# Eight experts in slots of 96 tokens: up weights in rows of 896 columns, gate and up in bank pairs, and POOL's share moved

## The reference

```python
logits = (t @ w_router).astype(jnp.float32) + b_router     # t: 256 tokens x 1024
top_v, top_e = lax.top_k(logits, 2)
gate = jax.nn.softmax(top_v, axis=-1)
...                                 # tokens sorted by expert, in blocks of up to 128
def one(args):                      # per expert: w_gate, w_up 1024 x 3584, w_down 3584 x 1024
    xb, e = args
    return (jax.nn.silu(xb @ w_gate[e]) * (xb @ w_up[e])) @ w_down[e]
...
y = zeros.at[row_tok].add(out * row_g)      # y[token] += gate * expert(token)
```

## Time and profile before

| | |
|---|---|
| median of 3 runs | 2813.24 us (2811.03 to 2813.75) |
| span of the profiled execution, first to last instruction | 2809.8 us |
| median less span | 3.4 us |
| PE, busy in the span | 2745.6 us, 98% |
| DVE | 1982.1 us, 71% |
| ACT | 1608.7 us, 57% |
| POOL | 700.7 us, 25% |
| first expert's first unit on TensorE | about 1876 us |
| last down matmul of the last expert | 2791.32 us |

### The profile page before, as it was taken

One profiled execution on the slowest core, in us unless ns is written; L12 is line 12 of the kernel. 1 busy time (PEld: TensorE's weight loads), 2 busy tenths in 40 slices (PEclk: granted clock), 3 DMA queues, 4 the chain that ended last, 5 costly groups with the idle time before them and its releaser, 6 DMA issues.

```text
span 2809.8 us, 68032 instructions
## 1 busy us (share of the span) xinstructions
PE 2745.6 (98%) x28028; PEld 2292.6 (82%) x28028; DVE 1982.1 (71%) x1914; ACT 1608.7 (57%) x1723; POOL 700.7 (25%) x562
## 2 busy tenths in 40 slices
PE   9999999999999999999999999999999999999997
PEld 7887788888877888887888887888879788797794
DVE  5457575564576755666855566778899898998986
ACT  5445663354356554455643445657677776777765
POOL 4314022122122221120122011144234243242331
PEclk9999999999999999999999999999999999999999
DMA  9764367576643676553576663469999999999995
GB/s 240 171 199 124 91 194 195 169 191 176 188 134 106 180 206 178 157 181 121 179 189 180 200 187 124 151 240 365 383 386 383 387 387 378 394 383 382 388 384 223
DMA packets 657516, 665.64 MB, mean 237 GB/s; under 512 B 25302, under 2 KB 513116, under 8 KB 657276
## 3 DMA queue, kind: packets, MB, share of 16 engines
q1 hardware_dynamic: 655696, 659.75, 71.5%
q0 software_dynamic: 704, 0.59, 0.4%
q10 hardware_dynamic: 876, 1.79, 0.2%
HBM read 661.01 MB, written 1.05 MB: 236 GB/s over the span
## 4 chain that ended last, share of the span: by engine, by line
PE 91%; DVE 4%; ACT 2%; issue 1%; DVEq 1%; DMA 0%; POOLq 0%; ACTq 0%; SPq 0%; POOL 0%
PE ps L2084 23%; PE ps L2085 23%; PE ps L2086 23%; PE ps L2814 3%; PE ps L2813 3%; PE ps L2812 3%; PE ps L2127 1%; PE ps L2133 1%; PE ps L2128 1%; DVE w_lo L1258 1%; PE ps L2437 1%; PE ps L2417 1%; ACT w_hi L705 1%; PE ps L2747 1%; PE ps L2505 1%
## 5 line engine op out<-in xcount | busy, mean ns | idle before, releaser
L2084 PE MATMUL ps<-x_hi,w_hi 128*128 128x128 f16 (+2 forms) x5440 | 1229.5, 250 | 16.1 <-DVE prod L1273 5.4
L2085 PE MATMUL ps<-x_lo,w_hi 128*128 128x128 f16 (+2 forms) x5440 | 1229.2, 250 | 0.0
L2086 PE MATMUL ps<-x_hi,w_lo 128*128 128x128 f16 (+2 forms) x5440 | 1229.0, 250 | 0.0
L1258 DVE SCALAR_TENSOR_TENSOR w_lo<-w,w_hi 128x2048 f16<-128x2048 f32 (+4 forms) x338 | 692.5, 2059 | 309.4 <-ACT w_hi L705 307.6
L705 ACT ACTIVATE w_hi<-w 128x2048 f16<-128x2048 f32 (+4 forms) x338 | 560.9, 1669 | 83.7 <-PE ps L2086 70.4
L2084 PEld LDWEIGHTS ps<-x_hi,w_hi 128*128 128x128 f16 x5440 | 534.0, 98 | 71.2 <-issue 14.4
L2085 PEld LDWEIGHTS ps<-x_lo,w_hi 128*128 128x128 f16 x5440 | 533.8, 98 | 45.9
L2086 PEld LDWEIGHTS ps<-x_hi,w_lo 128*128 128x128 f16 x5440 | 533.9, 98 | 42.6
L1754 DVE SCALAR_TENSOR_TENSOR w_lo<-w,w_hi 128x2048 f16<-128x2048 f32 x224 | 532.8, 2406 | 40.9 <-ACT w_hi L1178 40.8
L1178 ACT ACTIVATE w_hi<-w 128x2048 f16<-128x2048 f32 x224 | 416.9, 1901 | 28.4 <-DMA w<-in_moe_w_gate 12.0
L2066 POOL CAST ff<-pb 128x512 f16<-128x512 f32 x56 | 137.6, 2458 | 568.5 <-DVE pb L1846 568.5
(11 more groups left out here) (390 smaller groups left out, 4302.3 us busy)
## 6 DMA issues: line engine op xcount, KB each, us to landing
w<-in_ffn_w_up SPq DMA_DIRECT2D x176, 512.0 KB, 5.0
w<-in_moe_w_gate SPq DMA_DIRECT2D x80, 1024.0 KB, 8.1
w<-in_moe_w_up SPq DMA_DIRECT2D x80, 1024.0 KB, 8.7
...
w<-in_w_in SPq DMA_DIRECT2D x112, 512.0 KB, 4.6
...
```

The source lines that it names most:

```text
L1258: vec.scalar_tensor_tensor(k.w_lo[:, s, 0:size], k.w32[:, s, 0:size], WS, k.w_hi[:, s, 0:size], ALU.mult, ALU.subtract).then_inc(k.parts_r ...
L2084: pe.matmul(acc, w_hi, x_hi, start=first, stop=False)
L2085: pe.matmul(acc, w_hi, x_lo, start=False, stop=False)
L2086: return pe.matmul(acc, w_lo, x_hi, start=False, stop=last)
```

## The change

- **Slots for 96 tokens** (`CAP`), with up to three rounds (`ROUNDS`) for 128 and up to two. All that had 128 slots of tokens has 96: the moving columns of gather and up matmuls, the chunks of `a_hi3` and `a_lo3`, the rows of the expert's result.
- **Up weights in rows of 896 columns** (3584 bytes): 4 blocks of 7 chunks for 7 of 4. A unit holds two of the eight input chunks (`K_UNITS` = 4), so it is 128 x 1792 elements, 0.9175 MB and 42 matmuls, and a block has four gate units and then four up units, 32 units in all. The down part has 12 units as before and then four of one chunk (512 KiB), 16 in all. An expert has 48 units for 42.
- **Bank pairs.** A block's 7 x 96 results lie in two banks, chunks 128 columns apart. Gate takes one pair and up the other; the pairs change roles from one expert to the next (`gate_bank`), and the down sum lies in the gate's pair. `pa` and `pb` have room for one block. TensorE waits for silu before the next block's gate and for the product before the next block's up.
- **POOL's share.** The copy that makes `a_hi3` goes to ScalarE, one unit after the block's end; the subtraction that makes `a_lo3` to VectorE, two units after. POOL has no work in the experts.
- The loops over experts run over pairs of experts, since the bank numbers differ.

Places in the new kernel: `expert_split` of ScalarE is line 1201 and of VectorE line 1782; silu 1228, ScalarE's copy 1232, product 1874, subtraction 1879.

```diff
-BLOCK = 512
+BLOCK = 896
 BLOCKS = FFE // BLOCK
 BLOCK_CHUNKS = BLOCK // P
-UP_UNITS = 4 * BLOCKS
-DOWN_UNITS = EC // 2
+K_UNITS = 4
+UP_UNITS = 2 * K_UNITS * BLOCKS
+DOWN = [(2 * d, 2) for d in range(12)] + [(24 + d, 1) for d in range(4)]
+DOWN_UNITS = len(DOWN)
 E_UNITS = UP_UNITS + DOWN_UNITS
+HALF = D // 2
+
+
+CAP = 96
+ROUNDS = 3
...
+def unit_size(u):
+    return (KC // K_UNITS) * BLOCK if u < UP_UNITS else DOWN[u - UP_UNITS][1] * D
+
+
+def gate_bank(e):
+
+    return 2 * (e % 2)
+
+
+def chunked(banks, chunks):
+    return banks.rearrange("p b (c s) -> p (b c) s", s=P)[:, 0:chunks, 0:CAP]
...
+                w = (i["moe_w_gate_2"], i["moe_w_up_2"])[u // K_UNITS % 2][0][e]
+                some = KC // K_UNITS
+                expert_slot(u, q, some, BLOCK, chunks(w, u % K_UNITS * some, some, u // (2 * K_UNITS) * BLOCK, BLOCK))
+            for d, (ff, some) in enumerate(DOWN):
+                expert_slot(UP_UNITS + d, q, some, D, chunks(i["moe_w_down_2"][0][e], ff, some, 0, D))
...
-            b = u // 4 % 2
-            if u < UP_UNITS and u % 4 == 1:
+            block, step = u // (2 * K_UNITS), u % (2 * K_UNITS)
+            if u < UP_UNITS and step == K_UNITS - 1:
                 act.wait_ge(k.unit_done, q * E_UNITS + (E_FIRST + SLOTS + u + 1))
-                act.wait_ge(k.vec_evac, q * BLOCKS + (E_VEC + 2 + u // 4 - 1))
-                act.activation(k.e_silu[:, b, :], k.ps[:, 2 * b, :], ACT.Silu, scale=UNW).then_inc(k.silu_ready, 1)
+                act.wait_ge(k.vec_evac, q * BLOCKS + (E_VEC + 2 + block))
+                act.activation(k.e_silu, chunked(k.ps[:, gate:gate + 2, :], BLOCK_CHUNKS), ACT.Silu, scale=UNW).then_inc(k.silu_ready, 1)
+            if 0 < u <= UP_UNITS and step == 0:
+                rows = slice((block - 1) * BLOCK_CHUNKS, block * BLOCK_CHUNKS)
+                act.wait_ge(k.vec_evac, q * BLOCKS + (E_VEC + 2 + block))
+                act.activation(k.a_hi3[:, rows, :], k.e_prod, ACT.Copy).then_inc(k.ff_hi_ready, 1)
...
+            block, step = u // (2 * K_UNITS), u % (2 * K_UNITS)
+            if u < UP_UNITS and step == 2 * K_UNITS - 1:
                 vec.wait_ge(k.unit_done, q * E_UNITS + (E_FIRST + SLOTS + u + 1))
-                vec.wait_ge(k.silu_ready, q * BLOCKS + (E_GATES + u // 4 + 1))
-                vec.wait_ge(k.ff_ready, q * BLOCKS + (E_GATES + u // 4 + 1))
-                vec.scalar_tensor_tensor(k.e_prod[:, b, :], k.e_silu[:, b, :], UNW, k.ps[:, 2 * b + 1, :],
+                vec.wait_ge(k.silu_ready, q * BLOCKS + (E_GATES + block + 1))
+                vec.scalar_tensor_tensor(k.e_prod, k.e_silu, UNW, chunked(k.ps[:, up:up + 2, :], BLOCK_CHUNKS),
                                          ALU.mult, ALU.mult).then_inc(k.vec_evac, 1)
+            if 2 * K_UNITS <= u and block <= BLOCKS and step == 1:
+                rows = slice((block - 1) * BLOCK_CHUNKS, block * BLOCK_CHUNKS)
+                vec.wait_ge(k.ff_hi_ready, q * BLOCKS + block)
+                vec.tensor_tensor(k.a_lo3[:, rows, :], k.e_prod, k.a_hi3[:, rows, :], ALU.subtract).then_inc(k.ff_ready, 1)
...
-    def expert(q):
-        for block in range(BLOCKS):
-            b, rows = block % 2, slice(block * BLOCK_CHUNKS, (block + 1) * BLOCK_CHUNKS)
-            prod = k.e_prod[:, b, :].rearrange("p (c s) -> p c s", s=P)
-            pool.wait_ge(k.vec_evac, q * BLOCKS + (E_VEC + 2 + block + 1))
-
-            pool.sem_inc(k.pool_steps, 1)
-            pool.tensor_copy(k.a_hi3[:, rows, :], prod)
-            pool.drain()
-            pool.tensor_tensor(k.a_lo3[:, rows, :], prod, k.a_hi3[:, rows, :], ALU.subtract).then_inc(k.ff_ready, 1)
...
-            s, block, second = u % E_SLOTS, u // 4, u % 2
-            bank = 2 * (block % 2) + u // 2 % 2
+            s, block, step = u % E_SLOTS, u // (2 * K_UNITS), u % (2 * K_UNITS)
+            bank, v = gate if step < K_UNITS else 2 - gate, step % K_UNITS
             expert_weights(u)
-            if block >= 2 and u % 4 == 0:
-                pe.wait_ge(k.vec_evac, q * BLOCKS + (E_VEC + 2 + block - 1))
+            if block and step == 0:
+                pe.wait_ge(k.silu_ready, q * BLOCKS + (E_GATES + block))
+            if block and step == K_UNITS:
+                pe.wait_ge(k.vec_evac, q * BLOCKS + (E_VEC + 2 + block))
             for c in range(BLOCK_CHUNKS):
-                for kc in range(half):
+                for kc in range(some):
                     w = slice(kc * BLOCK + c * P, kc * BLOCK + (c + 1) * P)
-                    a = parts(k.ps[:, bank, c * P:(c + 1) * P], k.e_hi[s][:, w], k.e_lo[s][:, w],
-                              k.x_hi[:, second * half + kc, 0:P], k.x_lo[:, second * half + kc, 0:P],
-                              second == 0 and c == 0 and kc == 0, second == 1 and c == BLOCK_CHUNKS - 1 and kc == half - 1)
+                    a = parts(k.ps[:, bank + c // 4, c % 4 * P:c % 4 * P + CAP], k.e_hi[s][:, w], k.e_lo[s][:, w],
+                              k.x_hi[:, v * some + kc, 0:CAP], k.x_lo[:, v * some + kc, 0:CAP],
+                              v == 0 and c % 4 == 0 and kc == 0, v == K_UNITS - 1 and c in (3, BLOCK_CHUNKS - 1) and kc == some - 1)
...
+        for d, (first_ff, chunks) in enumerate(DOWN):
             u = UP_UNITS + d
             s = u % E_SLOTS
             expert_weights(u)
             if d == 0:
-                pe.wait_ge(k.vec_evac, q * BLOCKS + (E_VEC + 2 + BLOCKS - 1))
-            if 2 * d % BLOCK_CHUNKS == 0:
-                pe.wait_ge(k.ff_ready, q * BLOCKS + (E_GATES + 2 + d // 2 + 1))
-            for c in range(2):
-                ff = 2 * d + c
+                pe.wait_ge(k.silu_ready, q * BLOCKS + (E_GATES + BLOCKS))
+            for c in range(chunks):
+                ff = first_ff + c
+                if ff % BLOCK_CHUNKS == 0:
+                    pe.wait_ge(k.ff_ready, q * BLOCKS + (E_GATES + 2 + ff // BLOCK_CHUNKS + 1))
                 for n in range(2):
-                    acc, w = k.ps[:, 2 + n, :], slice(c * D + n * BLOCK, c * D + (n + 1) * BLOCK)
+                    acc, w = k.ps[0:CAP, gate + n, :], slice(c * D + n * HALF, c * D + (n + 1) * HALF)
                     pe.matmul(acc, k.a_hi3[:, ff, :], k.e_hi[s][:, w], start=ff == 0, stop=False)
                     pe.matmul(acc, k.a_lo3[:, ff, :], k.e_hi[s][:, w], start=False, stop=False)
                     a = pe.matmul(acc, k.a_hi3[:, ff, :], k.e_lo[s][:, w], start=False, stop=ff == EC - 1)
```

More of the change, by code:

```diff
@@ L690, in sp_program @@
     with sp.If(more > 0):
-        moe_round(1)
+        for r in range(1, ROUNDS):
+            moe_round(r)
 def act_program(act, k, i, out):
@@ L1228, in moe_round @@
             act.wait_ge(k.lo_gathered, 1)
-            act.activation(k.x_lo[:, :, 0:P], gathered(SPREAD[0] + 2), ACT.Copy).then_inc(k.xe_ready, 1)
-        with act.Fori(0, EXPERTS - 1) as e:
-            expert(r, e, last=False)
-        expert(r, EXPERTS - 1, last=True)
+            act.activation(k.x_lo[:, :, 0:CAP], chunked(k.ps[:, SPREAD[0] + 2:SPREAD[0] + 4, :], KC), ACT.Copy).then_inc(k.xe_ready, 1)
+        with act.Fori(0, EXPERTS // 2 - 1) as pair:
+            for n in range(2):
+                expert(r, 2 * pair + n, gate_bank(n), last=False)
+        expert(r, EXPERTS - 2, gate_bank(0), last=False)
+        expert(r, EXPERTS - 1, gate_bank(1), last=True)
     moe_round(0)
@@ L1870, in moe_round @@
             take_gates(r)
-            take_gathered(r * EXPERTS)
-            with vec.Fori(0, EXPERTS - 1) as e:
-                expert(r, e, last=False)
-        else:
-            expert(0, 0, last=False, first=True)
-            with vec.Fori(1, EXPERTS - 1) as e:
-                expert(0, e, last=False)
-        expert(r, EXPERTS - 1, last=True)
+            take_gathered(r * EXPERTS, 0)
+            with vec.Fori(0, EXPERTS // 2 - 1) as pair:
+                for n in range(2):
+                    expert(r, 2 * pair + n, gate_bank(n), last=False)
+        else:
+            for n in range(2):
+                expert(0, n, gate_bank(n), last=False, first=n == 0)
+            with vec.Fori(1, EXPERTS // 2 - 1) as pair:
+                for n in range(2):
+                    expert(0, 2 * pair + n, gate_bank(n), last=False)
+        expert(r, EXPERTS - 2, gate_bank(0), last=False)
+        expert(r, EXPERTS - 1, gate_bank(1), last=True)
     moe_round(0)
@@ L2757, in add_expert, with expert @@
                 for n in range(2):
[L2758 to L2760 removed]
+                    a = pe.matmul(y[:, t * D + n * HALF:t * D + (n + 1) * HALF],
+                                  k.to_token[0:CAP, bass.ds(e, 1), t * P:(t + 1) * P].rearrange("p a t -> p (a t)"),
+                                  x[0:CAP, n * HALF:(n + 1) * HALF], start=False, stop=False)
         a.then_inc(k.sum_added_to, 1)
[L2763 removed]
+    def expert(r, e, gate, last, first=False):
         q = e + r * EXPERTS
         added = e + (r * (EXPERTS + 1) + 1)
[L2766 removed]
+        some = KC // K_UNITS
         pe.wait_ge(k.xe_ready, q + 1)
```

(16 more changed lines are left out.)

102 lines of the change are left out of this document (42 added, 60 removed).

## The result

The changed kernel takes 2778.0 us (median of four runs, 2773.6 to 2779.8) against 2813.5 us of the kernel before in the same session: ratio 0.9869, 95% interval 0.9856 to 0.9883. It is 35.5 us faster; 46 were predicted (2767, range 2748 to 2803). The profiled execution took 2779.8 us with a span of 2777.9, so its span lies 1.9 us under its own time; the timed median lies 0.1 us over that span, where it lay 3.4 over it before.

What follows compares the result with a forecast made beforehand. TensorE bounds before, the DMA after: 336.5 MB at 402 GB/s take 837 us, landing at 2737; with tail and first expert TensorE ends at 2745.5, 46 us earlier. Span 2764 plus 3.4 gives 2767 us, range 2748 to 2803.

Steps and rivals of the forecast that it cites:

- TensorE gives up the bound: Expert part: up matmuls of 96 columns take 42.3 ns for 55.6, so TensorE falls from 114.5 to 96.3 us an expert.
- The DMA is next, and the row sets its rate: Expert weights: 3584-byte rows move at 405 GB/s, between 387 and 408; the DMA then bounds at 110.1 us an expert.
- The gaps: Expert weight transfers: 1.1 us an expert added to the DMA's 109.0 us for time without transfer.
- The rival that it bounds: Experts: VectorE sets the pace, 113 us an expert with its waits, 2789 us in all; chance 0.13.
- the ring of the slower rival: Block ends: ScalarE's copy, VectorE's splits and slot freeing delay each other until the DMA runs dry; 2825 us, up to 2850; chance 0.11.
- the sign: Block ends: VectorE idling over 3 us behind ScalarE's copy would show the prediction wrong.
- Start and tail: Experts' ends: 17.3 MB moved by 1900 us; after the last landing at 2737, TensorE ends at 2742.5, before 3 us more.
- The 3 us added for the first expert: First expert, where the backlog is TensorE's: 3 us added, moving TensorE's end from 2742.5 to 2745.5 us.
- The sum: Whole expert part: TensorE ends at 2745.5 us against 2791.55, 46 us saved; span 2764, timed median 2767.
- Row length brings nothing: Up weights: longer rows stay at 387 GB/s, so an expert takes 113.5 us, 2793 in all; chance 0.09.
- no change: Up matmuls: 96 columns cost what 128 do, so an expert stays at 114.8 us, 2813 in all; chance 0.04.
- a second round: Experts: a token count over 96 would run the whole part again, some 850 us; chance next to nothing.

## Why the prediction was right, and where its sizes were off

- **TensorE gives up the bound.** Right. 42.3 ns a matmul predicted, 42.5 measured; the 96-column weight loads of the down part take 123 ns and stay hidden, its matmuls start 216 ns apart (2744.75 to 2746.91 us, ten steps). A further third off its up matmuls moved an expert by 0.7 us.
- **The DMA is next, and the row sets its rate.** Right: 405 predicted for 3584-byte rows, 404 measured, 408 in the down part, and 386 in the experiment with 2048-byte rows. The Trainium skill (DMA: Bandwidth & Descriptors, Specifications) has line rate from 512 bytes on. The 262 GB/s of the earlier trace rows and the 386 beside 404, all at a share over 1.00, disagree with it.
- **The gaps: the mis-sized term.** I took 1.1 us of gaps an expert; the changed kernel shows 2.2 in one hole, and 111.3 us in place of 110.1 from add to add. Over 7.6 experts that is 9 us. I had asked for three transfers in flight, a number that no row shows, and counted them in number and not in bytes. The half units halve what a transfer holds: moved to the front they took the hole along, spread out they still cost 1.8 us an expert, in part by way of ScalarE's copy, and in no order that was tried did the loss go.
- **VectorE.** 101.0 us predicted, 102.90 in the row. A split of 1792 is 1.94 us from start to start (2698.86 to 2700.80) for 1.93, with a length of 2.02 that never stretches: right. The rival that it bounds fell as stated, since 2.0 to 2.7 us more of it cost only 0.6; but it is not free either: the 0.87 us taken from it at the hole brought 0.4 to 0.8.
- **ScalarE.** 82.8 predicted, 87.40 in the row: off by 4.6 us, without effect on the sum. I had counted steps from start to start (1.58 us for 1792), but behind a wait for the DMA each split shows its whole length, 1.70. Its wait for VectorE's product was costed at nothing and is 0.58 us; the ring of the slower rival did not form in the changed kernel (VectorE idles 0.52 us behind the copy, for over 3 in the sign), and showed itself in a small form, 1.59 us, when the half units were moved.
- **POOL's share.** I booked it as no gain and no loss. It is that: 111.4 from add to add with POOL, 111.3 to 111.6 without.
- **Start and tail.** 17.3 MB by 1900 us predicted; 44 x 0.205 + 20 x 0.371 = 16.4, because the experts began 4.5 us late. At 402 GB/s the missing 0.9 MB are 2.2 us. The tail behind the last landing was 8.5 us instead of 5.5, as ScalarE's last split and TensorE's last down matmul show:

```profile
2751.32 1.06 ACT L1201 ACTIVATE ff<-mix 128x1024 f16<-128x1024 f32 x1 [0.24 <-DMA mix<-in_moe_w_down]
```
```profile
2759.43 0.38 PE L2833 MATMUL ps<-mix,ff 128*96 128x512 f16 x1
```

The chain of waits shows where TensorE last stood still:

```profile
2734.04 2.21 DVE w_lo L1782
2736.30 0.42 PE ps L2831
```

It waited until 2736.30 us for a low half that VectorE had made behind the last block's difference. From there seven whole units and four half ones are 9 x 12 x 215.8 ns = 23.3 us without a pause. A down unit costs TensorE 2.59 us and the DMA 2.57, so the delay can't be worked off there. The prediction had 1.5 us of backlog for it. The 3 us added for the first expert made up for that, which was luck.
- **The sum.** TensorE ends at 2759.8 us for 2745.5: 14 us late, of which 9 are gaps and 2 the start, and some 3 stay unassigned. The forecast of the time is off by only 11 because I had put the median 3.4 us above the span and it lies 0.1 above it. Each execution takes 1.8 or 1.9 us more than its own span, so the 3.4 was no property of the kernel, and this too was luck.
- **Row length brings nothing, no change, a second round.** The first two fell with the 404 GB/s and with the expert part; the third did not occur, the adds of eight experts stand in the trace once.

What is not settled: how much of the 110.5 us that stay when the half units are spread and VectorE is relieved is ScalarE's wait at the copy, where the pure rates give 109.0; and what makes TensorE's clock fall at 225 to 250 us in some of the profiles.
